# A decoder layer on one core: the gate columns' projection block in two passes instead of three, and its splits placed ahead of those of x

## The chip, the cores and the metric

One core of a Trainium2 chip (trn2) runs the whole program. The time is that of one execution on the device in microseconds; of several executions the median is given. The engines are TensorE (PE, matmul and transposes), VectorE (DVE), ScalarE (ACT), GpSimd (POOL) and SyncE (SP), which here issues most DMAs.

## The reference

One layer of a decoder trunk for 512 prompt tokens and 8 x 4 sample tokens (544 columns in all), width 1024, in float32. What the change touches is the first projection and the gates of the mLSTM mixer that come out of it:

```python
h = rmsnorm(x, g_mix)
z = jnp.einsum('btd,dn->btn', h, w_in)
qa, ka, va, oa, ia, fa, qb, kb, vb, qc, kc, vc, gates = jnp.split(z, SPLIT_IDX, axis=-1)
...
mix_a = (hd(qa), hd(ka) * HEAD_DIM ** -0.5, hd(va), ia + b_if[:H_A], fa + b_if[H_A:])
```

`ia` and `fa` are 4 columns each, columns 1024 to 1031 of `w_in`. After them come a chunkwise mLSTM, a dilated window attention, a block-sparse attention, the merge with sigmoid gates, `w_out`, and a SwiGLU feed-forward layer.

## The kernel before

Everything is kept transposed: channels on the 128 partitions, the 544 tokens along the free axis, split in a half 0 of 256 and a half 1 of 288 tokens. Weights arrive in loads of 256 columns (1 MB), three buffers deep (`raw`), and are used in blocks of 128 columns. A product keeps float32 accuracy by splitting both sides into a high and a low part, each in a format that TensorE reads in one pass: `w_hi` is ACT's rounded copy of the weights (`split_hi`, L430), `w_lo` is DVE's `raw - w_hi` (`split_lo`, L435), and in the same way `h_hi` (ACT, L1503) and `h_lo` (DVE, L2067) hold x times the norm's gain. `products` (L451) then makes three passes for each of 8 slices of the contraction and each half: `w_hi * h_hi`, `w_hi * h_lo`, `w_lo * h_hi`. So a block is 24 passes of 256 columns and 24 of 288. The root mean square of x isn't known yet when this begins; `rstd` multiplies each sum as it is taken out of its bank (`evac`, on DVE).

Blocks are numbered w = 0, 1, ... Block 0 holds the gates: it loads 32 columns of `w_in` from column 1024 (the four of `ia` are the first of them) and 96 from column 1028 (the four of `fa` are the first), so that `ia` comes out on partitions 0 to 3 and `fa` on partitions 32 to 35, and the other 120 columns are not used. `evac(0, half)` multiplies these two groups of four rows by `rstd` (L1552, L1553) into `i_row` and `f_row`. Then come blocks 1 and 2 (`qa`), 3 and 4 (`ka`), and so on.

Each engine has one program, written out by hand. A `Side` object weaves further work in between the blocks: a side program yields a time in units of blocks and is run when the block loop passes it. Inside it, `v.then` on DVE issues an instruction and waits for its end before the next, `v.do` doesn't wait. The start is a fixed order on each engine:

- PE: transposes of x (L1154 tiles 0 and 1, L1167 the sample tile, L1154 tiles 2 and 3), then block 0, which waits for `w_lo_done`, for `h_lo` and for some copies of x; at time 1.3 (15 passes into block 1) five matmuls of `diag` (L848) that spread 1/rms over all partitions; at 2.1 the bias rows (L855, L856). At L868 the first transposes of `ka` wait for `evac(3, 1)`.
- ACT: sum of squares of tile 0, `x_hi(0)` (8 x L1503), the sample copy (L1519), `split_hi(0)`, squares of tiles 1 and 2, `x_hi(1)`, `split_hi(1)`, two copies (L1242), the last squares, the square root (L1244), `split_hi(2)`, the copies of `rstd` (L1247, L1248), later Exp and Ln of the forget gate (L1279, L1280), and only then `split_hi(3)`.
- DVE: `x_lo(0)` (8 x L2067), a copy, the sample's `h_hi` (L2077), `split_lo(0)`, a copy, the sample's `h_lo` (L2083), two copies, `x_lo(1)`, `split_lo(1)`, two copies, reciprocal and `diag` (L1685, L1687), `evac(0, 0)`, `evac(0, 1)`, `split_lo(2)`, four gate operations (L1702 to L1705), `evac(1, ...)`, `split_lo(3)`, `evac(2, 0)`, the scans of the forget gate (L1709, L1710), bias tables, `evac(2, 1)`, `split_lo(4)`, `evac(3, 0)`, a second scan (L1712 to L1719), `evac(3, 1)` (L1571).
- SP: an identity, x tiles 0 and 1, load 0 in its two parts (L422), the sample tile, x tiles 2 and 3, load 1, constants, load 2; load n then waits until the blocks of load n - 3 are split.

Up to block 2 four accumulator banks are used in turn, afterwards two, so that block 3's half 1 must wait for `evac(2, 1)`.

Of the kernel before, what the change touches and what calls it, by code (L numbers as in the profile page):

```python
# [7 lines left out]
ALU = mybir.AluOpType  # L8
ACT = mybir.ActivationFunctionType
AXX = mybir.AxisListType.X  # L10
F32 = mybir.dt.float32
# [3 lines left out]
P = 128  # L15
D = 1024
KD = D // P
# [5 lines left out]
HD = 64  # L23
HA = 4
# [122 lines left out]
def build(nc, I, O, X):  # L147

    with ExitStack() as ctx:
# [6 lines left out]
        def sem(name):  # L156
            if name not in sems:
                sems[name] = ctx.enter_context(nc.semaphore(name))
            return sems[name]
# [31 lines left out]
        w_hi = keep("w_hi", [P, 2, 1024], F32R)  # L191
# [16 lines left out]
        i_row, f_row = m("i_row", [HA, T]), m("f_row", [HA, T])  # L208
        v_st = m("v_st", [P, 2, T])
# [99 lines left out]
        def two(ap, half):  # L309
            return ap[:, HALF[0] * half:HALF[0] + HALF[1] * half]  # L310


        w_in, w_gu, w_dn, w_out = I["w_in"][0], I["w_gate_up"][0], I["w_down"][0], I["w_out"][0]

        def rows(w, k0, k1, c0, n):
            return w[k0 * P:k1 * P, c0:c0 + n].rearrange("(k p) n -> p k n", p=P)

        loads = []
# [4 lines left out]
            blocks.extend((len(loads) - 1, kts, 2 * P, j * P) for j in range(2))  # L323


        loads.append(([(0, 0, rows(w_in, 0, KD, 1024, 32)), (0, 32, rows(w_in, 0, KD, 1028, 96))], P))
        blocks.append((0, KD, P, 0))
        for c in list(range(0, 1024, 256)) + list(range(N_QKV, N_GATE, 256)):
            add_load([(0, 0, rows(w_in, 0, KD, c, 256))], KD)
# [57 lines left out]
        for w in range(n_all):  # L387
# [9 lines left out]
            else:  # L397
                c, n = divmod((w - n_gu) % 6, 2)
# [6 lines left out]
        mm_done, acc_ev, w_hi_done, w_lo_done = sem("mm_done"), sem("acc_ev"), sem("w_hi_done"), sem("w_lo_done")  # L405

        def raw_block(w):
            load, kts, ncol, off = blocks[w]
            v = raw[:, load % 3, 0:kts * ncol].rearrange("p (k n) -> p k n", n=ncol)
            return v[:, :, off:off + P]  # L410

        def split_block(t, w):
            return t[:, w % 2, 0:blocks[w][1] * P].rearrange("p (k n) -> p k n", n=P)
# [10 lines left out]
        def split_hi(act, w):  # L424

            load = blocks[w][0]
            act.wait_ge(w_loaded[load % 3], loaded_count[load])
            if w >= 2:
                act.wait_ge(mm_done, mm_at[w - 1])
            nc.scalar.activation(split_block(w_hi, w), raw_block(w), ACT.Copy).then_inc(w_hi_done, 1)  # L430

        def split_lo(dve, w):

            dve.wait_ge(w_hi_done, w + 1)
            nc.vector.tensor_tensor(split_block(w_lo, w), raw_block(w), split_block(w_hi, w).bitcast(F32),  # L435
                                    ALU.subtract).then_inc(w_lo_done, 1)

        def products(pe, side, w, x_hi, x_lo, kx=0, part=None, late=False):

            hi, lo = split_block(w_hi, w), split_block(w_lo, w)  # L440
            order = [(g, k) for g in groups[w] for k in range(g[5], g[6])]
            if late:
                order = [o for o in order if o[1] < KD - 1] + [o for o in order if o[1] == KD - 1]
            for place, ((idx, bank, first, last, half, k0, k1), k) in enumerate(order):
                if k == k0 and first and before[idx] is not None:
                    pe.wait_ge(acc_ev, before[idx] + 1)
                side.until(w + place / len(order))
                if part is not None:
                    part(half, kx + k)
                for c, (a, b) in enumerate(((hi, x_hi), (hi, x_lo), (lo, x_hi))):  # L450
                    ins = nc.tensor.matmul(acc[:, bank, 0:HALF[half]], a[:, k, :], two(b[:, kx + k, :], half),  # L451
                                           start=first and k == k0 and c == 0,
                                           stop=last and k == k1 - 1 and c == 2)
                if k == k1 - 1:
                    ins.then_inc(mm_done, 1)

# [173 lines left out]
        with nc.Block() as blk:  # L630
# [603 lines left out]
            def _(act):  # L1234
                a = Steps(act, sem("act_step"))
# [263 lines left out]
                def x_hi(half):  # L1499

                    for k in range(KD):
                        act.wait_ge(sem("x_tr"), 4 * half + k // 2 + 1)
                        nc.scalar.activation(h_hi[:, k, HB * half:HB * (half + 1)], x_bank(k, half), ACT.Copy,  # L1503
                                             scale=vecs[:, k:k + 1]).then_inc(sem("h_hi_done"), 1)
# [9 lines left out]
                act.wait_ge(sem("pool_set"), SET["ssx"])  # L1514
                squares(0)
                act.wait_ge(sem("vecs_done"), 1)
                x_hi(0)
                act.wait_ge(sem("xs_tr"), 1)
                nc.scalar.copy(xT[:, :, TP:T], acc[:, 7, 0:KD * TS].rearrange("p (k n) -> p k n", n=TS)).then_inc(sem("xs_ev"), 1)  # L1519
                split_hi(act, 0)  # L1520
                squares(1), squares(2)
                x_hi(1)
                side = Side(rstd_rows(), turn(), mlstm(), dilated(), attention(), gates(), sample(), sample_softmax(), merge(), feed())
# [17 lines left out]
            def _(dve):  # L1541
                v = Steps(dve, sem("dve_step"))

                def evac(w, half):

                    if w < n_proj:
                        name, i = kinds[w]
                        idx, src, ready = summed(w, half)
                        dve.wait_ge(mm_done, ready)
                        r = two(rstd, half)  # L1550
                        if name == "if":
                            v.do(nc.vector.tensor_tensor(two(i_row, half), src[0:HA], r[0:HA], ALU.mult))  # L1552
                            v.then(nc.vector.tensor_tensor(two(f_row, half), src[32:32 + HA], r[32:32 + HA], ALU.mult))  # L1553
                            nc.vector.nop().then_inc(acc_ev, 1)
                            return
                        if name[0] == "v":
# [26 lines left out]
                    elif w < n_merge and info[w][0] == "gate":  # L1583
                        _, j, r = info[w]
                        idx, src, ready = summed(w, half)
# [9 lines left out]
                    elif w < n_merge:  # L1595

                        k = info[w][1]
                        g, n = gs[(k // 2) % 2], k % 2
                        for c in ((0,) if half == 0 else (1, 2)):
# [5 lines left out]
                            for hf in range(2):  # L1605
                                idx, src, ready = summed(w, 2 * c + hf)
# [5 lines left out]
                    elif w < n_wout:  # L1612
                        k = w - n_merge
                        idx, src, ready = summed(w, half)
# [7 lines left out]
                    elif w < n_gu:  # L1622
                        j, r = divmod(w - n_wout, 4)
# [8 lines left out]
                        idx, src, ready = summed(w, half)  # L1632
# [7 lines left out]
                    else:  # L1640
                        j, r = divmod(w - n_gu, 6)
# [420 lines left out]
                def x_lo(half):  # L2062

                    for k in range(KD):
                        dve.wait_ge(sem("h_hi_done"), KD * half + 2 * (k // 2) + 2)
                        sl = slice(HB * half, HB * (half + 1))
                        nc.vector.scalar_tensor_tensor(h_lo[:, k, sl], x_bank(k, half), vecs[:, k:k + 1],  # L2067
                                                       h_hi[:, k, sl].bitcast(F32), ALU.mult, ALU.subtract).then_inc(sem("h_lo_done"), 1)

                def x_kept(b):  # L2070

                    nc.vector.tensor_copy(*x_pair(b)).then_inc(sem("xt_dve"), 1)

                x_lo(0)
                x_kept(0)
                dve.wait_ge(sem("xs_ev"), 1)
                nc.vector.tensor_tensor(h_hi[:, :, TP:T], xT[:, :, TP:T], vecs[:, 0:KD].unsqueeze(2).broadcast_to([P, KD, TS]),  # L2077
                                        ALU.mult).then_inc(sem("xs_hi"), 1)
                split_lo(dve, 0)
                x_kept(1)  # L2080
                dve.wait_ge(sem("xg_made"), 1)
                dve.wait_ge(sem("xs_hi"), 1)
# [59 lines left out]
```

## Time and profile before

| | us |
|---|---|
| median of 3 runs | 1001.25 (1000.13 to 1001.4) |
| the profiled execution | 1001.37 |
| its span, first to last instruction | 999.6 |
| PE busy | 976.0 (98%) |
| DVE busy | 489.0 (49%) |
| ACT busy | 337.6 (34%) |

The table shows the busy time of an engine over the whole span. In the rows below, a time is in microseconds from the span's start, L451 is line 451 of the kernel, and `out<-in` names the tiles that an instruction writes and reads. A PE row's duration is longer than its share, since matmuls overlap: the pace is read from start to start.

### The profile page before, as it was taken

Reading aid. Unit: us, or ns where it says so; the run is one execution under the profiler, and the core shown is the slowest. Engines: PE = TensorE matmul, PEld = TensorE weight load, DVE = VectorE, ACT = ScalarE, POOL = GpSimd, SP = SyncE. Lnnn points to the kernel's source line nnn. Section 1 sums busy time; section 2 is a strip of 40 time slices with the busy share of each in tenths; the row PEclk is TensorE's granted clock in tenths of the full one; section 3 lists DMA queues with packets and bytes.
Section 4 is the critical chain, followed back from the end, with each engine's and each line's share of the span. In section 5 each row is a group of like instructions: output and inputs, shape, how many; then the busy total and the mean of one; then the engine's idle time right before and its main releaser. Section 6 shows DMA issues by size and latency. Waiting matters only on the chain.

```text
span 999.6 us, 18273 instructions
## 1 busy us (share of the span) xinstructions
PE 976.0 (98%) x7624; PEld 950.6 (95%) x7624; DVE 489.0 (49%) x884; ACT 337.6 (34%) x577; POOL 74.3 (7%) x104
## 2 busy tenths in 40 slices
PE   7999999999999999899999999999999999999997
PEld 6899989999988889899999999999999999999997
DVE  5735566444877123544455565555544555323232
ACT  7343223444643441322222342322222222222222
POOL 0100022011201200111113000000000000000000
PEclk9999999999999999999999999999999999999999
DMA  7596336322220764322222222222222322222302
GB/s 250 131 273 232 73 89 152 109 85 77 98 65 2 221 208 125 94 85 85 86 85 85 86 85 85 85 85 85 88 95 99 99 86 75 85 75 77 114 1 90
DMA packets 104845, 105.03 MB, mean 105 GB/s; under 512 B 11074, under 2 KB 101688, under 8 KB 104428
## 3 DMA queue, kind: packets, MB, share of 16 engines
q1 hardware_dynamic: 101224, 92.78, 30.0%
q0 software_dynamic: 3488, 11.08, 3.6%
q8 instruction: 61, 1.00, 0.4%
q14 instruction: 20, 0.16, 0.0%
q10 hardware_dynamic: 52, 0.01, 0.0%
HBM read 98.00 MB, written 15.45 MB: 113 GB/s over the span
## 4 chain that ended last, share of the span: by engine, by line
PE 89%; DVE 5%; issue 1%; ACT 1%; POOL 1%; SPq 1%; DMA 1%; ACTq 0%; DVEq 0%; POOLq 0%
PE acc L451 75%; PE acc L1105 2%; PE acc L1054 1%; PE acc L1141 1%; POOL mt L827 1%; PE acc L1030 1%; DVE w_lo L435 1%; PE acc L1088 1%; PE acc L908 1%; PE acc L897 1%; SPq L681 1%; PE acc L868 1%; PE acc L1014 1%; PE acc L1229 1%; PE acc L1042 1%
## 5 line engine op out<-in xcount | busy, mean ns | idle before, releaser
L451 PE MATMUL acc<-h_hi,w_hi 128*128 128x256 f32 (+1 forms) x1520 | 465.9, 306 | 0.9 <-DVE w_lo L435 0.5
L451 PE MATMUL acc<-h_lo,w_hi 128*128 128x256 f32 (+1 forms) x1520 | 438.4, 288 | 0.0
L451 PE MATMUL acc<-h_hi,w_lo 128*128 128x256 f32 (+1 forms) x1520 | 436.5, 287 | 0.0
L451 PEld LDWEIGHTS acc<-h_hi,w_hi 128*128 128x128 f32 x1520 | 286.6, 189 | 9.0 <-issue 4.2
L451 PEld LDWEIGHTS acc<-h_lo,w_hi 128*128 128x128 f32 x1520 | 287.0, 189 | 4.8 <-issue 2.4
L430 ACT ACTIVATE w_hi<-raw 128x1024 fp32r<-128x1024 f32 x135 | 141.4, 1047 | 441.8 <-PE acc L451 441.7
L451 PEld LDWEIGHTS acc<-h_hi,w_lo 128*128 128x128 f32 x1520 | 286.9, 189 | 0.0
L435 DVE TENSOR_TENSOR w_lo<-raw,w_hi 128x1024 fp32r<-128x1024 f32 x135 | 165.6, 1226 | 112.5 <-ACT w_hi L430 107.7
L451 PE MATMUL acc<-s_hi,w_hi 128*128 128x256 f32 (+1 forms) x352 | 101.6, 288 | 0.0
L451 PE MATMUL acc<-s_lo,w_hi 128*128 128x256 f32 (+1 forms) x352 | 101.3, 288 | 0.0
L451 PE MATMUL acc<-s_hi,w_lo 128*128 128x256 f32 (+1 forms) x352 | 100.7, 286 | 0.0
L451 PEld LDWEIGHTS acc<-s_hi,w_lo 128*128 128x128 f32 x352 | 66.3, 188 | 0.0
L451 PEld LDWEIGHTS acc<-s_lo,w_hi 128*128 128x128 f32 x352 | 66.1, 188 | 0.0
L451 PEld LDWEIGHTS acc<-s_hi,w_hi 128*128 128x128 f32 x352 | 66.0, 187 | 0.0
L1635 DVE TENSOR_TENSOR sq<-acc,rstd 128x256 f32<-128x256 f32 (+1 forms) x44 | 19.2, 439 | 58.6 <-PE acc L451 58.6
L1594 DVE TENSOR_TENSOR gs<-acc,rstd 128x256 f32<-128x256 f32 (+1 forms) x48 | 21.1, 440 | 48.5 <-PE acc L451 47.3
L1635 DVE TENSOR_TENSOR sg<-acc,rstd 128x256 f32<-128x256 f32 (+1 forms) x44 | 19.4, 441 | 47.6 <-PE acc L451 46.9
L451 PE MATMUL acc<-y_hi,w_hi 128*128 128x288 f32 (+1 forms) x128 | 37.0, 289 | 1.6 <-DVE gs L1594 1.6
L451 PE MATMUL acc<-mg_hi,w_hi 128*128 128x288 f32 (+1 forms) x128 | 37.2, 291 | 1.4 <-issue 1.0
L451 PE MATMUL acc<-y_lo,w_hi 128*128 128x288 f32 (+1 forms) x128 | 36.9, 288 | 0.0
L451 PE MATMUL acc<-y_hi,w_lo 128*128 128x288 f32 (+1 forms) x128 | 36.9, 288 | 0.0
L451 PE MATMUL acc<-mg_lo,w_hi 128*128 128x288 f32 (+1 forms) x128 | 36.9, 288 | 0.0
(333 smaller groups left out, 1121.1 us busy)
## 6 DMA issues: line engine op xcount, KB each, us to landing
raw<-in_w_in SPq DMA_DIRECT2D x25, 1024.0 KB, 5.2
raw<-in_w_gate_up SPq DMA_DIRECT2D x22, 1024.0 KB, 4.9
raw<-in_w_down SPq DMA_DIRECT2D x8, 1024.0 KB, 4.8
rev<-tab POOLq DMA_DIRECT2D x1, 4352.0 KB, 18.7
ring<-in_cache_dsa_kv SPq DMA_DIRECT2D x4, 1024.0 KB, 6.5
raw<-in_w_out SPq DMA_DIRECT2D x4, 1024.0 KB, 4.8
out<-in_cache_dsa_kv SPq DMA_DIRECT2D x2, 2016.0 KB
ring<-in_cache_moba_k SPq DMA_DIRECT2D x48, 64.0 KB, 2.0
```

Of the source, the lines that this page charges most:

```text
L430: nc.scalar.activation(split_block(w_hi, w), raw_block(w), ACT.Copy).then_inc(w_hi_done, 1)
L435: nc.vector.tensor_tensor(split_block(w_lo, w), raw_block(w), split_block(w_hi, w).bitcast(F32), ALU.subtract).then_inc(w_lo_done, 1)
L451: ins = nc.tensor.matmul(acc[:, bank, 0:HALF[half]], a[:, k, :], two(b[:, kx + k, :], half), start=first and k == k0 and c == 0, stop=last ...
L681: sp.dma_start(ring[n % 4][:, m, :], src[:, P * (q - 3):P * (q - 2)]).then_inc(ring_in[n % 4], 16)
L827: st.then(nc.gpsimd.tensor_tensor(mt[:, 0, :], mt[:, 0, :], gated_part(k, c), ALU.add))
L868: ins = nc.tensor.transpose(acc[:, 2, P * i:P * (i + 1)], src[:, P * i:P * (i + 1)], ident)
L897: nc.tensor.matmul(acc[:, 3 + u % 3, 0:TP - P * i], zp[:, h % 2, P * i:P * (i + 1)], qT[:, h // 2, P * i:TP], start=True, stop=True).then_ ...
L908: nc.tensor.matmul(acc[:, 7, (HD + 1) * j:(HD + 1) * (j + 1)], PT[:, o:o + P], va_tok[:, s, h, :], start=s == 0, stop=s == j)
L1014: ins = nc.tensor.matmul(acc[:, 7, c:c + P], v, p, start=not near(t) or k == 0, stop=not near(t) or k == nk - 1)
L1105: nc.tensor.matmul(acc[:, 3 + q % 3, 2 * P - w:2 * P], Qpad[:, q // 3, b, :], KTs[:, n % 2, 0:w], start=b == 0 and q % 3 not in [o % 3 for ...
L1594: nc.vector.tensor_tensor(two(gs[j % 2][:, r, :], half), src, two(rstd, half), ALU.mult).then_inc(acc_ev, 1)
L1635: nc.vector.tensor_tensor(two(dst, half), src, two(rstd, half), ALU.mult).then_inc(acc_ev, 1)
```

## The change

The load of block 0 takes 32 columns instead of 96 for its second part, so the weights of both parts are in columns 0 to 63. ACT rounds those 64 columns into columns 0 to 63 of the `w_hi` tile, and DVE writes their low parts into columns 64 to 127 of the same tile. One pass over the tile then gives the high part's product on partitions 0 to 63 and the low part's on 64 to 127, so that block 0 makes two passes (with `h_hi` and with `h_lo`) where there were three. `evac(0, ...)` first copies partitions 64 to 99 of the bank to `v_st`, adds partitions 0 to 35, and multiplies the result by `rstd`. `split_hi(0)` stands ahead of `x_hi(0)` on ACT, `split_lo(0)` ahead of `x_lo(0)` on DVE.

```diff
-        loads.append(([(0, 0, rows(w_in, 0, KD, 1024, 32)), (0, 32, rows(w_in, 0, KD, 1028, 96))], P))
+        loads.append(([(0, 0, rows(w_in, 0, KD, 1024, 32)), (0, 32, rows(w_in, 0, KD, 1028, 32))], P))
...
-            nc.scalar.activation(split_block(w_hi, w), raw_block(w), ACT.Copy).then_inc(w_hi_done, 1)
+            c = HD if w == 0 else P
+            nc.scalar.activation(split_block(w_hi, w)[:, :, 0:c], raw_block(w)[:, :, 0:c], ACT.Copy).then_inc(w_hi_done, 1)
...
+            if w == 0:
+                both = split_block(w_hi, w)
+                nc.vector.tensor_tensor(both[:, :, HD:P], raw_block(w)[:, :, 0:HD], both[:, :, 0:HD].bitcast(F32),
+                                        ALU.subtract).then_inc(w_lo_done, 1)
+                return
...
-                for c, (a, b) in enumerate(((hi, x_hi), (hi, x_lo), (lo, x_hi))):
+                passes = ((hi, x_hi), (hi, x_lo)) if w == 0 else ((hi, x_hi), (hi, x_lo), (lo, x_hi))
+                for c, (a, b) in enumerate(passes):
...
+                split_hi(act, 0)
                 x_hi(0)
                 act.wait_ge(sem("xs_tr"), 1)
                 nc.scalar.copy(xT[:, :, TP:T], acc[:, 7, 0:KD * TS].rearrange("p (k n) -> p k n", n=TS)).then_inc(sem("xs_ev"), 1)
-                split_hi(act, 0)
...
-                            v.do(nc.vector.tensor_tensor(two(i_row, half), src[0:HA], r[0:HA], ALU.mult))
-                            v.then(nc.vector.tensor_tensor(two(f_row, half), src[32:32 + HA], r[32:32 + HA], ALU.mult))
+                            both = two(v_st[:, 0, :], half)
+                            v.then(nc.vector.tensor_copy(both[0:36], src[HD:HD + 36]))
+                            v.then(nc.vector.tensor_tensor(both[0:36], src[0:36], both[0:36], ALU.add))
+                            v.do(nc.vector.tensor_tensor(two(i_row, half), both[0:HA], r[0:HA], ALU.mult))
+                            v.then(nc.vector.tensor_tensor(two(f_row, half), both[32:32 + HA], r[32:32 + HA], ALU.mult))
...
+                split_lo(dve, 0)
                 x_lo(0)
                 x_kept(0)
...
-                split_lo(dve, 0)
                 x_kept(1)
```

How the instructions stand now. First ACT's queue from the end of the sum of squares of tile 0; `w_hi` is the weights' high part, `h_hi` that of x. Before:

```order
L1497 ACTIVATE xsq,ssx<-x_tok 128x1024 [waits x_in0,pool_set]
L1503 ACTIVATE h_hi<-acc,vecs 128x256 [waits x_tr,vecs_done,act_step]
L1503 ACTIVATE h_hi<-acc,vecs 128x256 [waits x_tr] x7
L1519 COPY xT<-acc 128x8x32 [waits xs_tr]
L430 ACTIVATE w_hi<-raw 128x1024 [waits w_loaded0]
L1497 ACTIVATE xsq,ssx<-x_tok 128x1024 [waits x_in1]
```

and after the change:

```order
L1504 ACTIVATE xsq,ssx<-x_tok 128x1024 [waits x_in0,pool_set]
L431 ACTIVATE w_hi<-raw 128x8x64 [waits w_loaded0,vecs_done,act_step]
L1510 ACTIVATE h_hi<-acc,vecs 128x256 [waits x_tr] x8
L1527 COPY xT<-acc 128x8x32 [waits xs_tr]
L1504 ACTIVATE xsq,ssx<-x_tok 128x1024 [waits x_in1]
```

The high part of the gates' weights stands ahead of the eight instructions on x and is half as long; its wait for the weights' load (`w_loaded0`) now holds up x too.

Second DVE's queue between the last `diag` (L1687, L1697) and block 2's low part. Before:

```order
L1687 TENSOR_SCALAR diag<-con,ssx 128x128 x4
L1552 TENSOR_TENSOR i_row<-acc,rstd 4x256 [waits mm_done,rstd_done]
L1553 TENSOR_TENSOR f_row<-acc,rstd 4x256
L1552 TENSOR_TENSOR i_row<-acc,rstd 4x288 [waits dve_step,mm_done]
L1553 TENSOR_TENSOR f_row<-acc,rstd 4x288
L435 TENSOR_TENSOR w_lo<-raw,w_hi 128x1024 [waits dve_step,w_hi_done]
```

and after the change:

```order
L1697 TENSOR_SCALAR diag<-con,ssx 128x128 x4
L1560 COPY v_st<-acc 36x256 [waits mm_done,rstd_done]
L1561 TENSOR_TENSOR v_st<-acc,v_st 36x256 [waits dve_step]
L1562 TENSOR_TENSOR i_row<-v_st,rstd 4x256 [waits dve_step]
L1563 TENSOR_TENSOR f_row<-v_st,rstd 4x256
L1560 COPY v_st<-acc 36x288 [waits dve_step,mm_done]
L1561 TENSOR_TENSOR v_st<-acc,v_st 36x288 [waits dve_step]
L1562 TENSOR_TENSOR i_row<-v_st,rstd 4x288 [waits dve_step]
L1563 TENSOR_TENSOR f_row<-v_st,rstd 4x288
L441 TENSOR_TENSOR w_lo<-raw,w_hi 128x1024 [waits dve_step,w_hi_done]
```

Four instructions are added in front of block 2's `w_lo`, and the first of them carries the wait for `rstd`.

## Rows read from the trace of the kernel before

**Rows 1.** The page, part 1: busy us of each engine, share, instructions.
```profile
PE 976.0 (98%) x7624; PEld 950.6 (95%) x7624; DVE 489.0 (49%) x884; ACT 337.6 (34%) x577; POOL 74.3 (7%) x104
```
**Rows 2.** Waits of PE, first 120 us: us in total, times, longest.
```profile
PE acc L868 <- DVE kT L1571: 0.6, 1, 0.6
```
**Rows 3.** Chain that ended last, 20 to 50 us: start, us, what.
```profile
27.39 0.41 DVE i_row L1552
27.81 0.03 issue
...
29.47 1.23 DVE w_lo L435
...
31.10 0.41 DVE rA L1703
...
35.48 0.96 ACT w_hi L430
...
36.46 1.23 DVE w_lo L435
...
47.48 0.66 PE acc L868 x4
```
**Rows 4.** Timeline of PE, 15 to 42 us: start, us, instruction, [idle before].
```profile
15.69 0.58 PE L451 MATMUL acc<-h_hi,w_hi 128*128 128x256 f32 x1 [0.55 <-DVE w_lo L435]
...
19.06 0.41 PE L451 MATMUL acc<-h_hi,w_hi 128*128 128x256 f32 x1
19.27 0.37 PE L451 MATMUL acc<-h_lo,w_hi 128*128 128x256 f32 x1
19.47 0.28 PE L451 MATMUL acc<-h_hi,w_lo 128*128 128x256 f32 x1
19.59 0.28 PE L451 MATMUL acc<-h_hi,w_hi 128*128 128x256 f32 x1
...
20.30 0.30 PE L451 MATMUL acc<-h_hi,w_hi 128*128 128x288 f32 x1
...
23.50 0.28 PE L451 MATMUL acc<-h_hi,w_hi 128*128 128x256 f32 x1
...
25.27 1.39 PE L848 MATMUL acc<-diag,ones 128*128 128x128 f32 x10
...
30.95 0.28 PE L451 MATMUL acc<-h_hi,w_hi 128*128 128x256 f32 x1
...
41.66 0.40 PE L451 MATMUL acc<-h_hi,w_hi 128*128 128x288 f32 x1 [0.33 <-DVE qT L1572]
```
**Rows 5.** Timeline of DVE, 14 to 25 us, the same columns.
```profile
14.41 1.22 DVE L435 TENSOR_TENSOR w_lo<-raw,w_hi 128x1024 fp32r<-128x1024 f32 x1
15.55 0.69 DVE L2072 COPY xT<-acc 128x512 f32<-128x512 f32 x1
...
20.81 1.22 DVE L435 TENSOR_TENSOR w_lo<-raw,w_hi 128x1024 fp32r<-128x1024 f32 x1
...
23.63 1.07 DVE L1687 TENSOR_SCALAR diag<-con,ssx 128x128 f32<-128x128 f32 x5
```
**Rows 6.** Timeline of ACT, 9 to 14 us, the same columns.
```profile
9.38 3.02 ACT L1503 ACTIVATE h_hi<-acc,vecs 128x256 fp32r<-128x256 f32 x8 [1.18 <-PE acc L1154]
...
12.50 1.13 ACT L430 ACTIVATE w_hi<-raw 128x1024 fp32r<-128x1024 f32 x1
13.46 1.12 ACT L1497 ACTIVATE xsq<-x_tok 128x1024 f32<-128x1024 f32 x1
```
**Rows 7.** DMA issues: count, KB each, us from issue to landing.
```profile
raw<-in_w_in SPq DMA_DIRECT2D x1, 384.0 KB, 6.3
```
**Rows 8.** SP's timeline at 2.6 us: load 0, second part.
```profile
2.63 0.58 SPq L422 DMA_DIRECT2D raw<-in_w_in  x1
```
**Rows 9.** DVE's forms, 13 to 50 us: count, busy us, mean ns, idle.
```profile
L2072 DVE COPY xT<-acc 128x512 f32<-128x512 f32 x6 | 3.9, 686 | 0.0
...
L1553 DVE TENSOR_TENSOR f_row<-acc,rstd 4x288 f32<-4x288 f32 x1 | 0.4, 448 | 0.0
```

More of the change, by code:

```diff
@@ L449, in products @@
                     part(half, kx + k)
-                for c, (a, b) in enumerate(((hi, x_hi), (hi, x_lo), (lo, x_hi))):
+                passes = ((hi, x_hi), (hi, x_lo)) if w == 0 else ((hi, x_hi), (hi, x_lo), (lo, x_hi))
+                for c, (a, b) in enumerate(passes):
                     ins = nc.tensor.matmul(acc[:, bank, 0:HALF[half]], a[:, k, :], two(b[:, kx + k, :], half),
                                            start=first and k == k0 and c == 0,
-                                           stop=last and k == k1 - 1 and c == 2)
+                                           stop=last and k == k1 - 1 and c == len(passes) - 1)
                 if k == k1 - 1:
```

## The prediction

> **What bounds the kernel now.** I began with the page's busy times: PE works 976.0 of 999.6 us [rows 1], so nothing but PE's work and its few waits can move the end, and a pass that is removed counts only if PE isn't made to wait for something else instead. Next I read PE's waits over the first 120 us, where the change sits. Besides the start there are three: 0.55 us ahead of block 0 for `w_lo` and 0.33 us at 41.66 for `qT` (both on PE's timeline, [rows 4]), and 0.6 us at the transposes L868 for `kT` [rows 2]. The last two are waits for DVE, some 20 us behind the change. The chain of waits says what they mean [rows 3]: it runs over PE up to L848, then leaves PE at 27.39, when DVE takes the gate sums, and follows DVE and ACT (gate rows, `w_lo` of block 2, more gate rows, Exp and Ln on ACT, ACT's `w_hi` at 35.48, `w_lo` at 36.46, the scans) until it comes back to PE at 47.48. Between 27.39 and 47.48 DVE's order sets the pace and PE is a little ahead of it. A gain on PE before that stretch reaches the end only as far as it makes the stretch begin earlier, and what DVE gets to do at its head is paid in full.
>
> **PE, block 0.** Today it starts at 15.69, after idling 0.55; its pace is 0.21 us a pass of 256 columns up to 19.4 (19.06 to 19.27) and 0.12 after (19.47 to 19.59), which are the clock's levels of 1.2 and 2.4 GHz; from 20.30 to 23.50 the 24 passes of 288 take 0.133 each, and the 15 passes of block 1 ahead of L848 take 1.77 (23.50 to 25.27) [rows 4]. Afterwards `w_lo` is no longer waited for, so block 0 starts at 15.14. Half 0 has 16 passes: 16 x 0.213 = 3.4, to 18.55. Half 1 has 16 of 288 columns; with the clock rising at 19.4 as now, 3.5 of them take 0.24 (0.213 x 288/256) and 12.5 take 0.133, together 2.5, to 21.05. Then 1.8 for the 15 passes, and PE reaches L848 at 22.85 instead of 25.27. Were the clock to rise at another time in an execution, both kernels would have it; it moves blocks 0 and 1 of both by about the same.
>
> **ACT and DVE ahead of L848.** Moving `w_hi` and halving it frees 0.96 us of ACT between L1519 and the squares (12.50 to 13.46) [rows 6]; all later ACT work up to the square root comes 0.96 earlier. In its new place it needs about 0.6 us ahead of `x_hi(0)`, where ACT idles 1.18 today [rows 6]: free, if the weights are there. The second part of load 0 is issued at 2.63 [rows 8] and lands 6.3 us later, at 8.93 [rows 7]; with a third of the bytes it lands between 4.7 (2.63 and a third of 6.3) and 8.93 (no gain at all). Up to 8.8 it is free (8.8 + 0.6 = 9.4, when the first transposed x is there), and nearly all of that span lies below 8.8, so I take it as free. On DVE the move frees 1.14 us (14.41 to 15.55) [rows 5] and the shorter `w_lo` falls into DVE's idle time before `x_lo(0)`: cost nothing, and if that cover were gone, 0.7. So `x_lo(1)` and `w_lo` of block 1 (today 20.81 to 22.03, [rows 5]) come 1.14 earlier, end at 20.89, and just don't delay block 1 at 21.05. `diag`, behind ACT's square root, starts at 23.63 today [rows 5] and then at 22.67; its first of five is ready at about 22.95. That is now later than PE (22.85): **L848 moves from 25.27 to 23.0, 2.27 earlier**, and `rstd` with it. SP's load 3, which waits for block 0's `w_lo`, is issued some 4 us earlier and queues behind load 2 on the same queue; its data isn't used before block 5, and nothing in the first 40 us waits for weights, so it costs nothing.
>
> **DVE, taking the gates.** Added in front of the stretch that sets the pace: a copy and an addition per half, over 36 partitions, of 256 and 288 elements, each waited for. No row shows such a copy. The nearest are the takings out of the same banks (L1553, 0.448 for 288 elements [rows 9]; L1552, 0.41 for 256 [rows 3]), each followed by 0.03 before the next starts [rows 3]. I take these: 2 x 0.44 + 2 x 0.48 = **1.84 us**, since source, length and waits are the same. The two multiplications stay as they are. Lower end: L1703 paces at 0.41 for 544 elements [rows 3], single-source and from SBUF; four at that price for half the elements, if time went by elements alone, 0.8. Upper end: the copy of 512 elements on 128 partitions, 0.686 [rows 9], four times with 0.03 each, 2.9. I stay with 1.84, since L1552 and L1553 are the nearest in source, length and few partitions.
> What the row shows is 0.412 for 256 elements out of the bank (27.39 to 27.81, [rows 3]). The Trainium skill ("VectorE: DVE Perf Modes", section "The TRN2 errata — SBUF-src ops pay a fixed extra latency per instruction") gives 120 cycles plus one per element at 0.96 GHz for an operation out of PSUM: an estimate of 0.39 and 0.43, 1.6 for the four, and a gain of 0.6 in place of 0.4. The measured row is 0.02 above it, so I keep the row. The same page ("Why PSUM operands drop a tier") has float32 out of PSUM run at one element per cycle at most, by which the lower end would be out of reach for the copies.
>
> **The sum.** The pace-setting stretch starts 2.27 earlier and is 1.84 longer: **0.4 us gained**. What PE gained beyond that turns into waits. Block 2 could start at 30.95 - 2.27 = 28.7 [rows 4], but `w_lo` of block 2, which today starts at 29.47 [rows 3], starts at 29.0 and ends at 30.3: PE gets a new wait of 1.6 us there, where it has none today. The waits at 41.66 and 47.48 stay about as they are, each 0.4 earlier. Behind 47.48 PE has work without a gap and the later waits hang on PE's own results, so 0.4 is what reaches the end. The profiled execution took 1001.37, against a median of 1001.25: 1001.0 for a profiled one, **1000.9** for the median. What the measurement of this kernel can tell from no change is about 0.2%, 2.0 us; the three runs lie 1.27 apart.
>
> **Rivals.**
> A. *PE's gain comes through whole* (8%). If DVE's order had slack, the 2.27 would stay: 999.0, faster by a little over 0.2%. It would need the four operations to cost next to nothing, or `w_lo` of block 2 not to stand behind them. Against it: the two waits on DVE and the chain [rows 2 to 4].
> B. *The four DVE operations cost more than the earlier start gives* (12%). The place is DVE between `rstd` and `w_lo` of block 2; it decides from 2.27 / 4 = 0.57 us for each with its wait. At the upper end of 2.9 it is 0.65 slower than before: 1001.9. For it: 36 partitions are read from partition 64 on and written to partition 0, which no row shows. Against: L1552 and L1553 already read partitions 0 and 32 at a plain price.
> C. *ACT waits for the weights and the early split doesn't help* (10%). If load 0 lands at 8.93 as now, `w_hi` ends near 9.6, and `x_hi(0)` and all of ACT's chain lose 0.2: L848 gains 2.05, the end 0.2: 1001.1. To eat the whole 0.4 the load would have to land at 9.1, later than now with a third of the bytes.
>
> **How the numbers follow.** 70% for the forecast: 1000.9. The range: below, the cheap bound of the four operations (0.8) would gain 1.5, 999.8, and some of the runs' spread makes it 999.5; above, B's 1001.9, with as much of the spread, 1002.2. A lies outside. Faster by over 0.2% is A alone, 0.08. Slower by over 0.2% needs B at more than one us an operation, 0.03. The rest, 0.89, is within 0.2%.
>
> **What would show it.** Right: PE starts block 0 near 15.1 with no wait for `w_lo`; L848 near 23.0 with a short wait for `diag`; DVE's four additions at 0.41 to 0.45; a PE wait of about 1.6 for `w_lo` at block 2 near 30.3; the transposes L868 near 47.1. Wrong: no wait at block 2 and L868 near 45.2 (A), additions of 0.6 and more (B), ACT idle ahead of `w_hi` and `x_hi(0)` later than 9.4 (C), or a part of the 0.4 lost or doubled behind 47 us, which would mean that PE isn't alone in setting the later time.

## The result, and the profile after

| | before | after the change |
|---|---|---|
| median, 7 runs each on one chip | 1001.4 (999.94 to 1003.55) | 1005.31 (1002.58 to 1008.95) |
| the profiled execution | 1001.37 | 1007.19 |
| its span | 999.6 | 1005.3 |

The ratio is 1.0033, with an interval of 1.0021 to 1.0044: slower by 3 to 4 us, above the range given. In a second series (`after_again`, below) it was 1.0016 (1.0002 to 1.0031). Both intervals lie above 1, so the change is slower. The size is less sure: 3.3 and 1.6 us by the two ratios, 3.9 and 2.6 by the medians.

The page of the changed kernel, part 1, against [rows 1]: 16 passes fewer, and PE is nevertheless busy for 2.4 us more.

```profile
PE 978.4 (97%) x7608; PEld 951.9 (95%) x7608; DVE 490.0 (49%) x888; ACT 337.4 (34%) x577; POOL 74.5 (7%) x104
```

Up to 30 us the forecast can be checked line by line. ACT's timeline (start, us, instruction, [idle before]): the early `w_hi` is free, and x follows it, when the transposes are ready.

```profile
8.22 0.63 ACT L431 ACTIVATE w_hi<-raw 128x512 fp32r<-128x512 f32 x1
9.29 3.03 ACT L1510 ACTIVATE h_hi<-acc,vecs 128x256 fp32r<-128x256 f32 x8 [0.44 <-PE acc L1161]
```

PE's timeline, the same columns, against [rows 4]: block 0 starts without a wait, the `diag` matmuls (L848 before, L855 now) at the forecast 23.0 and waiting for `diag`, then the forecast new wait for `w_lo`, and the transposes of `kT` (L868 before, L875 now) at 47.34, where 47.1 was forecast. The wait of 0.60 ahead of block 1 was not forecast ("just don't delay block 1"): in this execution the clock rose at 15.3, and PE was through with block 0 earlier.

```profile
14.78 0.56 PE L458 MATMUL acc<-h_hi,w_hi 128*128 128x256 f32 x1
...
20.77 0.39 PE L458 MATMUL acc<-h_hi,w_hi 128*128 128x256 f32 x1 [0.60 <-DVE w_lo L441]
...
23.03 1.46 PE L855 MATMUL acc<-diag,ones 128*128 128x128 f32 x10 [0.22 <-DVE diag L1697]
...
30.48 0.39 PE L458 MATMUL acc<-h_hi,w_hi 128*128 128x256 f32 x1 [1.53 <-DVE w_lo L441]
...
47.34 0.66 PE L875 MATMUL acc<-con,kT 128*128 128x128 f32 x4
```

DVE's timeline: the four added operations take 0.42 to 0.46 each and 0.45 to 0.50 from start to start: 1.89 us, where 1.84 was forecast.

```profile
25.24 0.43 DVE L1560 COPY v_st<-acc 36x256 f32<-36x256 f32 x1 [1.57 <-ACT rstd L1255]
25.70 0.42 DVE L1561 TENSOR_TENSOR v_st<-acc,v_st 36x256 f32<-36x256 f32 x1
26.15 0.41 DVE L1562 TENSOR_TENSOR i_row<-v_st,rstd 4x256 f32<-4x256 f32 x1
...
27.15 0.46 DVE L1560 COPY v_st<-acc 36x288 f32<-36x288 f32 x1
...
29.20 1.23 DVE L441 TENSOR_TENSOR w_lo<-raw,w_hi 128x1024 fp32r<-128x1024 f32 x1
...
72.23 0.18 DVE L1743 TENSOR_TENSOR ws<-by_tok,G 128x16 f32<-128x16 f32 x1 [5.37 <-DMA G<-gd]
```

The last of these lines is the surprise, 25 us behind everything that the forecast looked at. PE's waits of the first 120 us (us in total, times, longest) have it on top:

```profile
PE acc L879 <- ACT va_tok L1277: 2.4, 1, 2.4
PE acc L458 <- DVE w_lo L441: 2.1, 2, 1.5
```

The chain of waits of 44 to 90 us shows how it comes about (start, us, what). G, the gate row spread over all partitions (1 MB, issued by SP), takes 23.78 us from issue to landing; `ws` on DVE waits for it, ACT's `ws` for that, and behind ACT's `ws` in its queue stands the copy `va_tok` that PE needs.

```profile
46.77 1.57 DMA gd<-scan
...
48.36 23.78 DMA G<-gd
...
72.23 0.20 DVE ws L1743
...
72.51 0.03 ACT ws L1299
...
72.63 0.58 ACT va_tok L1277
73.21 0.04 issue
73.26 0.37 PE acc L879
```

In the kernel before, G had its own short wait, of which nothing reached PE (DVE's timeline, kernel before):

```profile
67.19 0.19 DVE L1733 TENSOR_TENSOR ws<-by_tok,G 128x16 f32<-128x16 f32 x1 [0.19 <-DMA G<-gd]
```

And the windows of the changed kernel (busy us and instructions by engine; then the granted TensorE clock as a share of full speed, DMA share, GB/s). Each of these stretches has a granted clock of 1.00 in the kernel before:

```profile
30.00:35.00 5.00, 4.52 (x21) 3.35 (x22) 3.15 (x7) 2.48 (x3) 0.00 (x0) 0.74 0.69 217
35.00:40.00 5.00, 5.00 (x38) 5.00 (x38) 3.74 (x5) 1.41 (x3) 0.00 (x0) 0.92 0.91 101
70.00:75.00 5.00, 2.59 (x15) 2.35 (x14) 1.96 (x5) 2.03 (x6) 0.00 (x0) 0.83 0.43 154
75.00:80.00 5.00, 5.00 (x27) 4.25 (x26) 2.52 (x7) 2.73 (x6) 0.00 (x0) 0.83 1.08 397
285.00:290.00 5.00, 5.00 (x27) 4.38 (x26) 2.79 (x9) 1.67 (x4) 0.00 (x0) 0.66 0.24 57
```

Three times the clock goes to its 1.2 GHz level, for 3.4 us each: after the wait for `w_lo`, after the wait for G, and near 285 after a wait of 2.04 us of L1061 for ACT. (Both kernels have more of it in their last 11 us.) The kernel before has that last wait too, but no fall behind it:

```profile
279.92 0.71 PE L1054 MATMUL acc<-PTs,v_tok 128*128 128x128 f32 x4 [2.05 <-ACT PTs L1397]
```

I laid the same matmuls of both traces side by side, counted from the last one. The changed kernel is 0.13 ahead at 47.5, still so at 67, 2.4 behind at 70.8 (the wait for G), 4.0 behind after the half-clock stretch there, 5.6 behind after the one near 285, 5.9 at the end. So in this pair of executions all the loss lies behind 48 us; it will turn out that this depends on when the clock rose in the kernel before.

### The profile page after: what moved, and what is told of

Its sections match the earlier page's. It is cut to its first block, busy times and chain, and to the rows that moved or that the text cites. A ratio compares the mean times of both kernels' runs of the same rounds, so it can differ in the third digit from the quotient of the medians.

```text
span 1005.3 us, 18245 instructions
## 1 busy us (share of the span) xinstructions
PE 978.4 (97%) x7608; PEld 951.9 (95%) x7608; DVE 490.0 (49%) x888; ACT 337.4 (34%) x577; POOL 74.5 (7%) x104
## 4 chain that ended last, share of the span: by engine, by line
PE 86%; DVE 4%; DMA 4%; ACT 2%; issue 1%; POOL 1%; SPq 1%; ACTq 0%; DVEq 0%; POOLq 0%
PE acc L458 72%; DMA G<-gd 2%; PE acc L1112 2%; PE acc L1061 1%; PE acc L1148 1%; PE acc L1037 1%; POOL mt L834 1%; PE acc L1095 1%; PE acc L915 1%; PE acc L904 1%; SPq L688 1%; PE acc L1021 1%; PE acc L1236 1%; ACT h_hi L1510 1%; DMA ring<-in_cache_dsa_kv 1%
## 5 line engine op out<-in xcount | busy, mean ns | idle before, releaser
L431 ACT ACTIVATE w_hi<-raw 128x1024 fp32r<-128x1024 f32 (+1 forms) x135 | 140.9, 1043 | 443.4 <-PE acc L458 443.3
L441 DVE TENSOR_TENSOR w_lo<-raw,w_hi 128x1024 fp32r<-128x1024 f32 (+1 forms) x134 | 164.1, 1225 | 112.6 <-ACT w_hi L431 107.8
L1645 DVE TENSOR_TENSOR sq<-acc,rstd 128x256 f32<-128x256 f32 (+1 forms) x44 | 19.2, 439 | 58.6 <-PE acc L458 58.6
L1645 DVE TENSOR_TENSOR sg<-acc,rstd 128x256 f32<-128x256 f32 (+1 forms) x44 | 19.4, 441 | 47.7 <-PE acc L458 46.9
```

What stands on the lines that cost most here:

```text
L431: nc.scalar.activation(split_block(w_hi, w)[:, :, 0:c], raw_block(w)[:, :, 0:c], ACT.Copy).then_inc(w_hi_done, 1)
L1645: nc.vector.tensor_tensor(two(dst, half), src, two(rstd, half), ALU.mult).then_inc(acc_ev, 1)
```

## The experiments

"Position at L868" is the start of PE's `kT` transposes (L868, L875 or one or two lines beside), 47.48 in the kernel before [rows 3]; "G" is its time from issue to landing, 18.6 us in the kernel before. The profiled execution of each run gives both; the ratio comes from all its runs, against 17 to 35 of the kernel before on the same chip.

**First, the two halves of the change.** `order_only` has the early splits and keeps three passes; `passes_only` has the two passes and keeps the old places of the splits.

```diff
 order_only, against the kernel before
+                split_hi(act, 0)
                 x_hi(0)
...
-                split_hi(act, 0)
...
+                split_lo(dve, 0)
                 x_lo(0)
...
-                split_lo(dve, 0)
```

> The early splits alone, three passes kept, DVE takes the gates as before. Theory G (the broadcast of the gate row G lands on one DMA engine 5 us later, since PE's 16 KB instruction fetch falls into its last part there; 32 PE instructions fewer moved it): PE's instructions are as many as before, so G lands near 67 and the median is 0 to 1 us below the kernel before. Theory C (the clock falls after the new PE wait ahead of block 2): no new wait ahead of block 2, no loss either, 0 to 1 us faster. Theory O (the moved splits, with load 3 issued earlier, are at fault): the loss of 3 to 4 us stays.

> The two passes and the four DVE operations alone, the splits where they were. Theory G: 32 PE instructions fewer as in the change, so G lands late on one engine in most executions, 3 to 4 us slower than before. Theory C: PE's wait ahead of block 2 is there too (about 1.5 us), so 3 to 4 us slower as well. Theory O: no loss. By the DVE chain alone the stretch to 47.5 us would be about 1 us later than in the change.

`order_only`: 1001.39, ratio 0.9991 (0.998 to 1.0003); L868 at 45.72; G 19.0. `passes_only` (the same edit backwards, against the changed kernel): 1003.59, ratio 1.0023 (1.0011 to 1.0035); L875 at 47.65; G 24.7, and PE's waits in its profile:

```profile
PE acc L879 <- ACT va_tok L1277: 3.2, 1, 3.2
PE acc L458 <- DVE w_lo L441: 2.1, 2, 1.5
```

The early splits alone are not slower, so they are not at fault; the two passes carry the loss, and the late G and the wait ahead of block 2 both come with them.

**Then, G.** `after_nops` puts 32 empty instructions at the head of PE's program, where it idles, to move its instruction fetches; `after_rev_late` lets the 4.3 MB transfer `rev` on POOL's queue wait until G is in. `before_nops` puts 224 of them into the kernel before. `after_again` is the change itself.

```diff
 after_nops (before_nops: 224)
+                for _ in range(32):
+                    nc.tensor.nop()
                 pe.wait_ge(sem("con_in"), 16)
...
 after_rev_late
                 pool.wait_ge(sem("tab_out"), 48)
+                pool.wait_ge(sem("g_in"), 16)
                 pool.dma_start(X["rev"]
```

> The change with 32 empty PE instructions at the head of PE's program, where it idles 6.6 us, so that PE's instruction stream is as long as before up to every later place. Theory G: the fetches fall where they fell before, G lands near 67.3, PE has no wait for va_tok near 71, median within 1 us of the kernel before. Theory C: nothing changes, 3 to 4 us slower than before, the wait ahead of block 2 and clock falls stay.

> The change with POOL issuing the 4.35 MB transfer rev only once G has landed, so G has the DMA engines nearly alone. Theory G: G lands within 6 us of its issue, near 54, the wait near 71 goes and the median is within 1 us of the kernel before, perhaps 0.5 faster. Theory C: 3 to 4 us slower stays, only the DMA times change.

> The kernel before with 224 empty instructions on TensorE's sequencer ahead of its first wait, near 2 us, where it has nothing to do. They shift TensorE's instruction fetches against the program by about as much as the change does, and nothing else. Theory G (a 16 KB instruction fetch that falls near 64 us on the DMA engine that carries the last packets of G makes G land 5 us late): G lands near 72 instead of 67, TensorE waits 2 to 4 us near 71, and the kernel is 1 to 4 us slower than before. If the fetch has nothing to do with it: G lands at 65.7 to 67.5 as in the kernels with three passes, and the time is that of before within 0.1%.

> The change once more, beside the next three on one chip. Theories G and C together (each takes a part): 2 to 4 us slower than before. If the loss is G alone, after_nops would have had none of it; it had 1.4, so I expect G lands near 72 again and the clock falls once or twice between 28 and 39 us.

`after_nops`: 1003.68, ratio 1.0014 (1.0005 to 1.0023), G 19.8, no wait at L879. `after_rev_late`: 1003.45, ratio 1.0015 (1.0004 to 1.0027), G 4.8, no wait. `after_again`: 1004.16, ratio 1.0016 (1.0002 to 1.0031), G 23.1, PE's wait 1.7:

```profile
G<-gd SPq DMA_DIRECT2D x1, 1024.0 KB, 23.1
```

```profile
PE acc L879 <- ACT va_tok L1277: 1.7, 1, 1.7
```

`before_nops`: 1001.59, ratio 0.9997 (0.9987 to 1.0007), G 19.1. Its 16 KB fetch fell at 58.6, not near 64 as in the changed kernel, so it didn't set up what it was to test. Read together: with G in time in their profiles, the two variants of the change still are 1.4 and 1.5 us slower than the kernel before by their ratios, with intervals above 1. For `after_nops` this says little, since its profile is of the fastest of its 11 executions (1000.47, against a median of 1003.68), and whether G was in time in the others isn't known. `after_rev_late` is the better witness: G is issued ahead of `rev` there, and its profile (1003.55) is near its median. Laid beside the kernel before, it is 1.3 us behind at 48 us and 1.4 at 300, with one long fall of the clock ahead of 48 (31.9 to 38.7):

```profile
35.00:40.00 5.00, 5.00 (x28) 5.00 (x28) 3.82 (x5) 1.08 (x2) 0.00 (x0) 0.63 0.90 97
```

So G is part of the loss and not all of it.

**What G's lateness is worth by itself.** `before_late_ws` gives it to the kernel before, whose DMAs and PE program stay as they are.

```diff
                     dve.wait_ge(sem("g_in"), 16)
+                    for n in range(18):
+                        v.then(nc.vector.tensor_tensor(diag[:, n % 4, :], ident, ident, ALU.mult))
                     v.then(nc.vector.tensor_tensor(ws[:, :].rearrange("p (i h) -> p i h", h=HA),
```

> The kernel before, with 18 idle products of 128x128 on VectorE (some 0.28 us each, 5 us in all) between the arrival of G, near 67, and ws; DMA and TensorE's program are untouched. It gives ws the lateness that it has in the changed kernel (72.2 instead of 67.2), without the late landing. Theory G (that lateness is the main loss of the change): TensorE waits 2 to 4 us near 71 and the kernel is 2 to 5 us slower, ratio 1.002 to 1.005, the more if a half-clock stretch follows. Rival (work behind takes it up, and C is the whole loss): within 0.1% of before.

1008.31, ratio 1.0065 (1.0052 to 1.0078), 6.65 us more. DVE's timeline: the products take 5.84, `ws` comes at 73.48, 6.3 later than before; then PE's waits; then two windows.

```profile
67.60 5.84 DVE L1734 TENSOR_TENSOR diag<-con 128x128 f32<-128x128 f32 x18 [0.67 <-DMA G<-gd]
73.48 0.18 DVE L1735 TENSOR_TENSOR ws<-by_tok,G 128x16 f32<-128x16 f32 x1
```

```profile
PE acc L872 <- ACT va_tok L1270: 3.6, 1, 3.6
```

```profile
75.00:80.00 5.00, 5.00 (x26) 4.39 (x25) 2.36 (x9) 2.84 (x6) 0.00 (x0) 0.74 1.04 383
285.00:290.00 5.00, 5.00 (x24) 4.43 (x25) 2.75 (x7) 1.67 (x4) 0.04 (x1) 0.66 0.44 105
```

It is the changed kernel's picture line for line: a wait of PE near 71, a stretch at half clock behind it, another near 285; the positions against the kernel before are -0.06 at 48, +3.7 at 70.8, +5.1 at 73 and +6.7 at 283. Such a lateness without two passes makes the same kind of loss (6.3 us late here, 5.0 in the changed kernel's profile), so this half of the mechanism is shown. Work behind 48 us does not take it up.

**The wait ahead of block 2.** Idle copies behind `i_row` and `f_row` make DVE later there, nine in `before_wait`, four in `before_wait_small`; `after_lo2` instead moves the changed kernel's `w_lo` of block 2 ahead of the wait for `rstd`.

```diff
 before_wait_small (before_wait: range(4 + half))
                             v.then(nc.vector.tensor_tensor(two(f_row, half), src[32:32 + HA], r[32:32 + HA], ALU.mult))
+                            for _ in range(2):
+                                v.then(nc.vector.tensor_copy(two(v_st[:, 0, :], half)[0:36], src[HD:HD + 36]))
...
 after_lo2, against the changed kernel
                         nc.vector.tensor_scalar(diag[:, i, :], ident, ssx[:, i:i + 1], None, ALU.mult).then_inc(sem("diag_done"), 1)
+                    split_lo(dve, 2)
                     dve.wait_ge(sem("rstd_done"), 2)
...
-                    if 1 <= w < n_all - 1:
+                    if 2 <= w < n_all - 1:
                         split_lo(dve, w + 1)
```

> The kernel before, whose program for TensorE is untouched; VectorE alone gets nine idle copies of 36 partitions (some 0.45 us each, 4.2 us in all) behind i_row and f_row, so that w_lo of the next block of weights ends near 34.9 instead of 30.7 and TensorE, which wants it near 33.1, waits 1.5 to 2 us there, as it does near 29 in the changed kernel. No other part of the change is in it. Theory C (a wait of this size is followed by stretches at half clock, and those are the loss): a new half-clock stretch behind 35 in the profile, mean granted clock near .995 as for the changed kernel, and 1.5 to 4 us more than before (ratio 1.002 or more). Theory of the prediction (such a wait is made good before 48 us, and nothing behind it changes): within 0.2 us at 48 us and a ratio of 1.000. A wait that is simply paid in full gives 1.5 to 2 us with no fall of the clock.

> The kernel before with four idle copies on VectorE instead of the nine of before_wait (there TensorE's wait at the next block was 3.9 us, a half-clock stretch from 32.7 to 42.9 followed, and the time rose by 5.9 us). Five copies fewer of 0.45 to 0.48 us leave a wait of about 1.6 us, the size of the changed kernel's own. Theory C (such a wait is paid, and a stretch at half clock behind it as well): 1.5 to 3.5 us more than before, ratio 1.0015 to 1.0035. Theory of the prediction (made good before 48 us): 1.000. If only long waits bring the clock down: the wait alone, 1.6 us at most, and no new half-clock stretch in the profile.

> The change with DVE making w_lo of block 2 ahead of the four added operations, in its idle time before rstd, so PE has no wait near 28.7. Theory C: the clock doesn't fall near 32 us, the stretch to 47.5 is 1.2 us shorter, G's lateness stays if theory G holds (PE's instruction count is that of the change): 1 to 3 us better than the change in the median. Theory G alone: no better than by that 1.2.

`before_wait`: 1007.4, ratio 1.0059 (1.0043 to 1.0074), with a wait twice as long as was meant. `before_wait_small`: 1005.69, ratio 1.0043 (1.003 to 1.0056), above what either theory gave. Their PE rows at block 2:

```profile
33.74 0.58 PE L451 MATMUL acc<-h_hi,w_hi 128*128 128x256 f32 x1 [3.94 <-DVE w_lo L435]
```

```profile
31.18 0.39 PE L451 MATMUL acc<-h_hi,w_hi 128*128 128x256 f32 x1 [1.55 <-DVE w_lo L435]
```

In `before_wait` the clock is at half for all of 35 to 40:

```profile
35.00:40.00 5.00, 5.00 (x17) 2.93 (x17) 2.00 (x4) 3.63 (x4) 0.00 (x0) 0.50 1.14 270
```

In `before_wait_small` no fall follows the wait (1.00 throughout 25 to 45), but one comes near 280 and some at the end. Its `kT` transposes start at 47.89, and that is 1.6 later than in `before_nops` (46.30), which had the same early clock; counted from PE's first matmul (6.29 and 6.59) it is 1.9. So four small DVE operations, 1.9 us, come through whole in this profile, without a fall of the clock. The other 2 us of its loss aren't explained. `after_lo2`: 1001.68, ratio 0.9999 (0.9987 to 1.0012), L875 at 46.43. The change is back at the time of before. Three things went at once, though: PE's wait ahead of block 2, one `w_lo` of the stretch on DVE, and the wait for G, which was issued 0.4 ahead of `rev` and landed after 4.6 us.

```profile
23.95 1.22 DVE L441 TENSOR_TENSOR w_lo<-raw,w_hi 128x1024 fp32r<-128x1024 f32 x1
25.60 0.43 DVE L1560 COPY v_st<-acc 36x256 f32<-36x256 f32 x1 [0.43 <-ACT rstd L1255]
```

**A better version.** `after_both` and `before_both` add both remedies (early `w_lo` of block 2, `rev` after G) to the changed kernel and to the one before; `order_lo2` is `order_only` with the early `w_lo`, run twice; `order_again` repeats `order_only`.

> The change with both remedies (w_lo of block 2 early, rev after G). If G and C are the whole loss: 1 to 1.5 us faster than the kernel before, near 1001.0 where before is 1002.3. If something else is lost too, it stays slower.

> The kernel before with the same two remedies. The DVE stretch from 27.4 to 47.5 is 1.2 us shorter, but PE leads there by only 1.2 us: 0.5 to 1.2 us faster than before. The two passes alone, told by after_both against this, are then worth what is left of 2.3 us.

> Three passes; the early splits of the change; and the low part of the second following block of weights also split early, ahead of the wait for rstd. TensorE's wait at that block isn't there in this kernel without the move either, so by theory C the move is worth nothing here: 0.998 to 1.000, as the early splits alone (0.9991). If the moved split delays VectorE's following rows by its 1.23 us and that reaches the end: 1.001.

> The early splits alone, with three passes, once more, since it was the fastest part at 0.9991 with an interval that touched 1. If the 0.9 us are real, 0.998 to 1.000 with a median near 0.999; if they were the chip's spread, 1.000 with an interval on both sides.

> The same as order_lo2 (three passes, early splits, the following low part early as well), which ran at 0.9988 with an interval that ended at 0.9999. If that gain is real: 0.998 to 0.9995 again; if it was the chip's spread: an interval around 1.

| run | median | ratio, interval | kT transposes |
|---|---|---|---|
| `after_both` | 1001.67 | 1.0006 (0.9993 to 1.0019) | 46.00 |
| `before_both` | 1000.63 | 0.9991 (0.9975 to 1.0007) | 46.46 |
| `order_again` | 1000.94 | 0.9996 (0.9986 to 1.0006) | 46.04 |
| `order_lo2` | 1000.37 | 0.9988 (0.9978 to 0.9999) | 44.84 |
| `order_lo2_again` | 1000.38 | 0.999 (0.998 to 1.0001) | 45.19 |

With G's wait gone and the stretch short, two passes are no faster than three. The two series of `order_lo2` agree on 0.10 to 0.12%, one interval just below 1 and one that reaches just above it: about 1 us faster than the kernel before is likely and not shown. `order_only` and its repeat can't be told from the kernel before. Contrary to what was expected, the moved split was worth something with three passes as well, on DVE's stretch: `kT` 45.0 against 45.9 on average over two profiles each. In the whole time that gain is not clear of the noise.

## Why the prediction was wrong

**Point by point.** Right, to 0.1 to 0.4 us: block 0's start without a wait, L848 at 23.0 and bound by `diag`, the four operations at 1.84, `w_lo` of block 2 (29.0 forecast, 29.20), the new wait of 1.6 (1.53), the transposes at 47.1 (47.34). Against the kernel before as it was profiled, the sum even held up to 48 us: 0.13 ahead, where 0.4 was forecast. Rival B (dearer operations) fell, and so did C (weights late). Rival A did not occur. Three steps failed; the second weighs the most.

**The first step that failed: "Were the clock to rise at another time in an execution, both kernels would have it; it moves blocks 0 and 1 of both by about the same."** It doesn't move both. In the profiled execution of before, PE still ran at half pace until 19.4 [rows 4]. In `before_nops` it was at full pace from block 0's second pass on (0.12 from start to start), though that block waited 1.64 for `w_lo`:

```profile
15.60 0.39 PE L451 MATMUL acc<-h_hi,w_hi 128*128 128x256 f32 x1 [1.64 <-DVE w_lo L435]
15.82 0.28 PE L451 MATMUL acc<-h_lo,w_hi 128*128 128x256 f32 x1
15.94 0.27 PE L451 MATMUL acc<-h_hi,w_lo 128*128 128x256 f32 x1
...
24.00 1.46 PE L848 MATMUL acc<-diag,ones 128*128 128x128 f32 x10
```

```profile
26.21 0.41 DVE L1554 TENSOR_TENSOR i_row<-acc,rstd 4x256 f32<-4x256 f32 x1 [1.57 <-ACT rstd L1250]
```

Here three passes reach L848 at 24.00, not 25.27, and DVE takes the gates at 26.21, not 27.39. The changed kernel can't use an early clock further, since `diag` binds its L848. How much that is worth is seen best when each time is counted from PE's first matmul, since the DMA that this one waits for lands anywhere between 6.3 and 7.6 us:

| run | clock at full from | gates taken, from PE's first matmul | from there to the `kT` transposes |
|---|---|---|---|
| kernel before | 19.5 | 20.72 | 20.09 |
| `before_late_ws` | 19.6 | 20.87 | 20.08 |
| `before_nops` | 10.5 | 19.62 | 20.09 |
| `before_wait_small` | 10.7 | 19.62 | 21.98 |
| `order_only` | 15.5 | 19.08 | 20.09 |
| `order_again` | 11.5 | 18.99 | 20.09 |
| `passes_only` | 11.0 | 19.19 | 21.98 |
| `after_again` | 11.0 | 18.58 | 21.95 |
| changed kernel | 15.3 | 18.59 | 22.10 |
| `after_rev_late` | 14.8 | 18.57 | 23.66 |

The last column is the stretch that DVE paces: 20.1 with three passes, 1.9 more with four more operations, whether they are the change's or idle ones. The term of 1.84 was right. The term of 2.27 was not: with an early clock the gates are taken 1.0 us earlier than in `before_nops` (18.57 to 18.60 in all six profiles with both halves of the change, against 19.62), with a late one 2.1 to 2.3. So in executions with an early clock the sum is a loss of 0.9 us and not a gain of 0.4, and the transposes say the same (counted from PE's first matmul, 0.8 later in `after_again` and 1.0 in the changed kernel than in `before_nops`). Of the six profiled kernels with the old start and three passes, three had the early rise and three the late one (19.5 to 19.7): the sum was made against one of two kinds of start, and the one that flattered the change. None of the other eleven profiles has the late rise, so how the changed kernel does with it wasn't seen. The two lowest rows also show what a fall of the clock does in this stretch: 3.4 us at half clock cost 0.1, since PE has slack there, and 6.8 us in `after_rev_late` cost 1.7. Against the profiled kernel before, that run gained 2.1 at the head and lost 1.9 and 1.7 in the stretch, which is its lag of 1.3 at 48 us.

**The second: "Behind 47.48 PE has work without a gap and the later waits hang on PE's own results, so 0.4 is what reaches the end."** Both halves are wrong. PE does have gaps there in the kernel before, among them 2.05 us at 279.92 and 1.59 at 416.47; I had looked at the first 120 us only. And the path from G's DMA over DVE and ACT to PE has no term in the sum, though G comes from DVE's rows. G doesn't show in PE's waits of before, because it landed just in time: DVE waited 0.19 for it and PE nothing. In all three two-pass profiles without empty instructions or another issue order, G took 23.1 to 24.7 us; in the eight three-pass profiles that issue `rev` and then G within 1 us it took 18.6 to 20.9. PE then waited 1.7 to 3.2 us. `before_late_ws` gives the price, 6.65 us for 6.3 us of lateness with its half-clock stretches; in the changed kernel's profile `ws` is 5.0 late and the place costs 4.1 up to 78 us, 1.55 of it by the half clock. Together with the 0.9 of the first step that makes more than the 2.6 to 3.9 that the medians show. That leaves room for executions in which G is in time or the clock doesn't fall.

**The third is what a stretch at half clock adds.** Where PE sets the pace, 3.4 us of it cost 1.4 to 1.6 us: 2.44 to 3.99 behind 70.8 and 4.0 to 5.6 near 283 in the changed kernel, 3.7 to 5.1 and 5.1 to 6.7 in `before_late_ws`. The prediction had no term for it. A wait of PE comes first, but it doesn't settle the matter: behind the wait ahead of block 2 the clock fell in the changed kernel (wait of 1.53) and not in `after_again` (1.54), which is the same kernel. The Trainium skill ("TensorE: Matmul & The Clock Gate", section "A second HAM failure mode: psum-queue depth-cycling") tells of a kernel in which frequent short idle times of TensorE made the clock swing between its two levels, and says that the swing cost throughput. The traces agree on the swing and on its cost; but here, ahead of the last 11 us, the falls come singly, behind or within single waits of 1.3 to 3.9 us.

The falls come more often with the change: of its 19 runs in two series, 3 have a mean granted clock of 0.998 or more and 11 one of 0.996 or less; of the 116 runs of the kernel before beside the experiments, it is 42 and 29. The same two groups of the kernel before have medians of 1000.5 and 1003.0, so the clock goes with its own spread too.

**What stays open.** Why G lands late in the two-pass kernels. The trace shows how: G's landing is told in 16 parts, which I take for the 16 DMA engines, and in the changed kernel fifteen were in at 67.3, the last of all in the kernel before at 67.1. The sixteenth came at 72.1. `after_again` and `passes_only` have the same picture, fifteen by 67.6 and 68.4 and one at 72.2 and 73.2. The only packets of G still under way then, two of 8 KB, ran from 67.1 to 71.6 in the changed kernel, while packets of 63,488 bytes of the cache copies (L659, SP's next issues) took 6.2 to 6.6 us each. In the kernel before these copies ran at the same time and as slowly, but G's last packet was through at 66.6. The Trainium skill ("DMA: Bandwidth & Descriptors", section "Queues, rings and completion order") says that a DMA engine takes turns between its queues packet by packet. That doesn't account for it here, since the trace has G's late packets and the cache copies on one queue. Why one engine was behind the other fifteen at all is not settled. The guess that PE's 16 KB instruction fetch does it is not borne out: the fetch fell at 63.9 in the changed kernel and at 64.0 in `passes_only`, but at 61.4 in `after_again`, where G was late, and at 61.0 in `after_nops`, where it was in time; `before_nops`, which should have tested it, didn't move the fetch to that place. How the 2.6 to 3.9 us divide over many executions between the shorter gain, G and the clock is open too; the runs show that the three steps take part, single profiles give their sizes. And why the clock rises early in one execution and late in another isn't known.

## What to carry to other kernels

A pass removed from the busiest engine is worth only what the next binding row lets through. Here the two passes and the early splits let a stretch that DVE paces begin 1.0 to 2.3 us earlier, and put 1.9 us of DVE's work at its head. Read the start of a kernel from several executions, or at both clock levels, before a difference is taken against it: the slower kernel may be the one that can use an early clock. And list the transfers that land within a microsecond of their use, since a wait of 0.19 us on an idle engine was the row that turned into 4 us. Count times at the head of a kernel from the same first instruction: over the six profiles with the whole change, a spread of 1.1 us in the time of the gates fell to 0.03 that way.

## What the runs showed of the hardware

In three profiles one part of 16 of a 1 MB transfer, one DMA engine's as I read it, came about 5 us after the other fifteen; the median over engines says nothing there, the last packet does. TensorE's clock at the head of the program first rose between 10.2 and 19.7 us over 17 executions of nearly the same start, and a wait of 1.5 us was followed by half clock in one execution of a kernel and not in the next. A stretch of 3.4 us at half clock cost 1.4 to 1.6 us where TensorE set the pace, and 0.1 where VectorE did.
